# Feed-forward of a two-layer transformer block: the down product moved behind the next group's first gate and up

## The reference

```python
def swiglu_sublayer(h, shift, scale, gate, w_g, w_u, w_d, g, b):
    u = modulate(h, shift, scale)
    f = (jax.nn.silu(u @ w_g) * (u @ w_u)) @ w_d
    return post_norm(h, f, gate, g, b)
```

## Time and profile before

| | us |
|---|---|
| median of 3 runs | 4003.86 (4000.16 to 4005.01) |
| span of the profiled execution | 3998.6 |
| PE busy in it | 3531.9 (88%) |
| DVE, ACT, POOL busy | 1602.3, 1449.1, 1662.3 |
| matmuls of the feed-forward start, layer 0 | 1247.9 |
| matmuls of the feed-forward start, layer 1 | 3235.2 |

### The profile page before, as it was taken

The page is one execution under the profiler, slowest core; times in us unless marked ns, Lnnn a source line. Parts: engine busy times, 40 slices in busy tenths (PEclk is TensorE's granted clock), DMA queues, the critical chain, the costliest instruction groups (busy, mean ns, idle before and its releaser), DMA issues. The chain is left out here.

```text
span 3998.6 us, 55066 instructions
## 1 busy us (share of the span) xinstructions
PE 3531.9 (88%) x21518; PEld 2912.4 (73%) x21518; DVE 1602.3 (40%) x2560; ACT 1449.1 (36%) x2423; POOL 1662.3 (42%) x1104
## 2 busy tenths in 40 slices
PE   6899598788797999999998699597988979999997
PEld 2588487566476888888887487486665768888886
DVE  2103454686583222224433204465855722223324
ACT  2311275685443111113332311375854432222221
POOL 1211142583333444445565211244933345555553
PEclk9999799798998999999999799698989989999998
DMA  8422310232242222223333223322343433333332
GB/s 302 164 88 110 124 41 14 69 69 56 83 148 86 64 64 64 64 64 106 101 112 105 93 87 112 101 47 62 73 143 103 162 106 96 95 95 111 111 100 94
DMA packets 171083, 388.52 MB, mean 97 GB/s; under 512 B 14536, under 2 KB 75048, under 8 KB 170864
## 3 DMA queue, kind: packets, MB, share of 16 engines
q1 hardware_dynamic: 148480, 334.24, 27.3%
q10 hardware_dynamic: 19904, 44.77, 3.0%
q0 software_dynamic: 2480, 6.48, 0.6%
HBM read 319.41 MB, written 66.03 MB: 96 GB/s over the span
## 5 line engine op out<-in xcount | busy, mean ns | idle before, releaser
L2375 POOL TENSOR_TENSOR ffn_wlo<-ffn_raw,ffn_whi 128x1024 fp32r<-128x1024 f32 x264 | 644.5, 2448 | 677.1 <-ACT ffn_whi L2287 677.1
L2287 ACT CAST ffn_whi<-ffn_raw 128x1024 fp32r<-128x1024 f32 x264 | 272.6, 1049 | 877.2 <-PE ffn_acc L127 464.7
L2509 DVE TENSOR_TENSOR ffn_silu<-ffn_up,ffn_silu 128x256 f32<-128x256 f32 (+1 forms) x143 | 75.4, 527 | 946.3 <-PE ffn_up L127 937.0
L125 PE MATMUL ffn_gate<-second_uhi,ffn_whi 128*128 128x256 f32 (+1 forms) x1144 | 375.4, 328 | 42.8 <-POOL ffn_wlo L2375 34.1
L126 PE MATMUL ffn_gate<-second_ulo,ffn_whi 128*128 128x256 f32 (+1 forms) x1144 | 374.6, 327 | 0.0
L127 PE MATMUL ffn_gate<-second_uhi,ffn_wlo 128*128 128x256 f32 (+1 forms) x1144 | 374.3, 327 | 0.0
L125 PE MATMUL ffn_up<-second_uhi,ffn_whi 128*128 128x256 f32 (+1 forms) x1144 | 370.9, 324 | 0.8 <-POOL ffn_wlo L2375 0.8
L126 PE MATMUL ffn_up<-second_ulo,ffn_whi 128*128 128x256 f32 (+1 forms) x1144 | 370.6, 324 | 0.0
L127 PE MATMUL ffn_up<-second_uhi,ffn_wlo 128*128 128x256 f32 (+1 forms) x1144 | 370.3, 324 | 0.0
L2521 DVE TENSOR_TENSOR y<-ffn_acc,y 128x512 f32<-128x512 f32 x360 | 248.2, 691 | 257.8 <-PE ffn_acc L127 257.8
L125 PE MATMUL ffn_acc<-ffn_whi,ffn_hhi 128*128 128x512 f32 x792 | 314.1, 397 | 22.4 <-DVE y L2521 21.2
(11 more groups left out here) (286 smaller groups left out, 7939.2 us busy)
## 6 DMA issues: line engine op xcount, KB each, us to landing
ffn_raw<-w_ffn_dram SPq DMA_DIRECT2D x264, 512.0 KB, 3.6
in_raw<-w_in_dram SPq DMA_DIRECT2D x42, 512.0 KB, 3.6
inputs_ada_w<-w_ada_dram SPq DMA_DIRECT2D x10, 2048.0 KB, 8.3
swa_ada_w<-w_ada_dram SPq DMA_DIRECT2D x8, 2048.0 KB
proj_scratch<-in_stage ACTq DMA_DIRECT2D x20, 640.0 KB, 2.9
ada_w<-w_ada_dram SPq DMA_DIRECT2D x6, 2048.0 KB
gla_kq<-proj_scratch SPq DMA_DIRECT2D x32, 320.0 KB, 7.7
local_qhl<-heads_scratch SPq DMA_DIRECT2D x36, 256.0 KB
```

Source lines behind the costliest of these rows:

```text
L125: pe.matmul(out, st_hi, mv_hi, start=start, stop=False)
L2287: act.copy(whi[:, w % 3, :], raw[:, w % 2, :]).then_inc(w_hi, 1)
L2375: pool.tensor_tensor(wlo[:, w % 3, :], raw[:, w % 2, :], whi[:, w % 3, :].bitcast(F32), ALU.subtract).then_inc(w_ready, 1)
L2509: dve.tensor_tensor(sg[:, n % 2, 0:tn], UP[:, n % 2, 0:tn], sg[:, n % 2, 0:tn], ALU.mult).then_inc(mul_done, 1)
```

## The change

The loops over passes and groups become one loop over q = 0 to 21. On PE the down product of step q-1 moves behind G0 and U0 of step q and ahead of G1 and U1 of step q; the last one stands alone at the end. The order in which the weight tiles are loaded, split and kept in the three slots is now G0, U0, D0 and D1 of the step before, G1, U1 (`order`). The hidden tiles get three slots in place of two. `alone` goes: all chunks are whole. Each engine's loop is rewritten to that order. The core of the diff:

```diff
-        def alone(chunk):
-            t0, tn = chunk
-            return [[(t0, tn)], [(t0, tn // 2), (t0 + tn // 2, tn // 2)]]
-        passes = [alone(CHUNKS[0]) if last else [[CHUNKS[0], CHUNKS[2]]] * 2, alone(CHUNKS[1])]
...
+        passes = [[CHUNKS[0]] if last else [CHUNKS[0], CHUNKS[2]], [CHUNKS[1]]]
+        WIDTH = sum(tn for _, tn in passes[0])
+        Q = 2 * G
+        HS = 3
...
-        hhi = sb(nm + "hhi", [P, 2, WIDTH], F32R)
-        hlo = sb(nm + "hlo", [P, 2, WIDTH], F32R)
+        hhi = sb(nm + "hhi", [P, HS, WIDTH], F32R)
+        hlo = sb(nm + "hlo", [P, HS, WIDTH], F32R)
...
+        def hidden_slot(q, f):
+            return (2 * q + f) % HS
...
+        GATE, UPPER, DOWN = (0, 2), (1, 3), (4, 5)
+        order = []
+        for q in range(Q):
+            order += [(q, GATE[0]), (q, UPPER[0])]
+            if q:
+                order += [(q - 1, j) for j in DOWN]
+            order += [(q, GATE[1]), (q, UPPER[1])]
+        order += [(Q - 1, j) for j in DOWN]
+        place = {name: w for w, name in enumerate(order)}
...
-            for j in range(3):
-                split(0, 0, j)
-            for p in range(2):
-                for g in range(G):
-                    k = norm_tile(p, g)
-                    turning = k is not None and not last
-                    if k is not None:
-                        deviation(k, 0)
-                    if turning:
-                        deviation(k, 1)
-                    silu(p, g, 0)
-                    split(p, g, 3)
-                    if turning:
-                        normalize(k)
-                    split(p, g, 4)
-                    silu(p, g, 1)
-                    split(p, g, 5)
-                    if following(p, g)[0] < 2:
-                        split(*following(p, g), 0)
-                    if turning:
-                        if k == 0:
-                            act.wait_ge(one_plus, 1)
-                        modulate(k)
-                    if following(p, g)[0] < 2:
-                        for j in range(1, 3):
-                            split(*following(p, g), j)
+            split(0, GATE[0])
+            split(0, UPPER[0])
+            for q in range(Q):
+                k = norm_tile(q)
+                turning = k is not None and not last
+                if k is not None:
+                    deviation(k, 0)
+                if turning:
+                    deviation(k, 1)
+                silu(q, 0)
+                if q:
+                    split(q - 1, DOWN[1])
+                split(q, GATE[1])
+                if turning:
+                    normalize(k)
+                split(q, UPPER[1])
+                if q + 1 < Q:
+                    split(q + 1, GATE[0])
+                if turning:
+                    if k == 0:
+                        act.wait_ge(one_plus, 1)
+                    modulate(k)
+                silu(q, 1)
+                if q + 1 < Q:
+                    split(q + 1, UPPER[0])
+                split(q, DOWN[0])
+            split(Q - 1, DOWN[1])
...
-            for j in range(3):
-                split(0, 0, j)
-            for p in range(2):
-                for g in range(G):
-                    if not last and norm_tile(p, g - 1) is not None:
-                        low_part(norm_tile(p, g - 1))
-                    split(p, g, 3)
-                    hidden(p, g, 0)
-                    split(p, g, 4)
-                    split(p, g, 5)
-                    hidden(p, g, 1)
-                    if following(p, g)[0] < 2:
-                        for j in range(3):
-                            split(*following(p, g), j)
+            split(0, GATE[0])
+            split(0, UPPER[0])
+            for q in range(Q):
+                if not last and norm_tile(q - 1) is not None:
+                    low_part(norm_tile(q - 1))
+                if q:
+                    split(q - 1, DOWN[1])
+                split(q, GATE[1])
+                hidden(q, 0)
+                split(q, UPPER[1])
+                if q + 1 < Q:
+                    split(q + 1, GATE[0])
+                    split(q + 1, UPPER[0])
+                hidden(q, 1)
+                split(q, DOWN[0])
+            split(Q - 1, DOWN[1])
...
+            for q in range(Q):
+                gate_and_up(q, 0)
+                if q:
+                    down(q - 1)
+                if norm_tile(q) is not None and not last:
+                    turn(norm_tile(q))
+                gate_and_up(q, 1)
+            down(Q - 1)
```

## The result

The changed kernel takes 4038.14 us (median of 4 runs, 4033.99 to 4040.42), the kernel before 4003.20 us (4 runs). The ratio is 1.0085, with a 95% interval of 1.0072 to 1.0099: slower by 34.9 us. That lies in the predicted range (4044 us, 4020 to 4063, slower). The profiled execution has a span of 4035.2 us, 36.6 above that of before.

What follows compares the result with a forecast made beforehand. Plain steps were taken as bound by PE's matmul stream, norm steps partly by something else. Terms -21.8 - 3.7 + 38.1 + 7.2 + 20.4 = +40.2 us on the 3998.6 us span, plus 5.3 to the median, gave 4044; range 4020 to 4063.

Steps and rivals of the forecast that it cites:

- whole chunks: In 33 steps, 96 matmuls of 256 columns become 48 of 512; each step 0.66 us shorter, 21.8 us gained.
- hidden tile in pass 0: In pass 0 of layer 0, PE no longer waits for the hidden tile just made; 11 x 0.34 = 3.7 us gained.
- six norm steps of layer 0: Down product waits 6.5 or 9.3 us for D1's split, which stands behind norm work; three pairs lose 38.1 us.
- four norm steps of layer 1: PE waits 1.8 us for D1's split in each of four steps, no clock loss charged; 7.2 us lost.
- two ends: Each layer's last down product waits 7.8 us for POOL, plus 2.4 us of clock; twice 10.2 = 20.4 us lost.
- Plain steps don't wait: In steps without norm work the weights arrive in time, with 1.0 us to spare for D1; steps of 32.64 us.
- rival (a): DVE's norm chain gets 2 us shorter, so ten norm steps wait less: 19 us back, 4025; chance 0.14.
- The clock: Behind long waits PE's clock falls to the 1.2 GHz level; 2.2 us lost in a norm step, 2.4 at an end.
- The transposes: Waits ahead of the transposes in norm steps of layer 0 cost 1.2 us a step, as before.
- (d): Rival for whole chunks: wider matmuls save nearly nothing, 17.5 us worse, 4062; chance 0.06 together with another rival.
- (b): Rival for norm steps: silu comes early enough that the norm chain doesn't hold D1; -28 us, 3976; chance 0.05.

Runs made afterwards that it cites:

- d1_cast_first: Changed kernel with D1's cast on ACT ahead of the step's square roots and silu, in place of behind them; 4005.15 us, ratio to the kernel before 1.0005.
- filler: Changed kernel with matmuls whose result nobody reads run on PE ahead of the eight long waits for D1; 4021.82 us, ratio to the kernel before 1.0043.
- tail_splits_first: Changed kernel with D0 and D1 split on POOL ahead of the hidden tile in each layer's last step; 4023.80 us, ratio to the kernel before 1.0046.
- before_whole: Kernel before with the second hidden tile in one piece of 512 columns, the down product not moved; 4128.27 us, ratio to the kernel before 1.0309.

## Why the prediction was right

In the feed-forward parts the change costs 34.8 us; the other 1.8 of the profile's 36.6 lie in stages it doesn't touch. The mechanism and the time both came out as forecast; two terms were off by 2 to 4 us. Point by point:

| term | predicted | measured in the trace |
|---|---|---|
| whole chunks, 33 x 0.66 | -21.8 | 0.66 in every plain step |
| hidden tile in pass 0, 11 x 0.34 | -3.7 | 0.31 to 0.33 a step |
| six norm steps of layer 0 | +38.1 | +34.7 |
| four norm steps of layer 1 | +7.2 | +5.1 |
| two ends | +20.4 | +20.9 |

The last three are against steps of 32.64 us; with 33 x 0.66 and 11 x 0.32 for the first two, the terms add up to 35.4 us, 0.6 above the 34.8. For layer 0 the six steps are 64.0 us over 32.64 now and were 29.3 over 33.30; the ends are 78.8 us from U1's end to the next stage's first matmul against 68.1, and 49.3 against 39.1.

- Plain steps don't wait: right. PE is never idle in them, and D1 is there in time.
- Norm steps: the mechanism is right and shown (d1_cast_first). The waits are 5.97 (once 6.76) and 8.35 us between matmuls, I had 6.5 and 9.3; in layer 1 1.04 (once 1.31), I had 1.8. The term was taken from the split in the same place of the kernel before. The difference is part of rival (a): DVE's second `residual` operation takes 1.52 us now, 3.30 before, and `shifted` then meets D0's split and takes 2.91, where 1.66 stood before. In the second step the low part of the normed tile falls on `shifted` (3.22 us for 1.29), against 2.9 us saved in `residual`. The chain came out 0.5 to 1.0 us shorter, not 2. In layer 1 the whole wait of 1.04 us is D1's split itself: it starts at 3662.91, behind a DVE operation that started at 3662.79, and takes 3.40 us where it takes 2.4 elsewhere.
- The clock: it fell in all eight long waits, 2.33 to 2.65 us in a norm step's down product, I had 2.2, and didn't fall after 0.88 us. The filler run shows it as a cost of its own.
- The transposes cost 0.9 us in a norm step and not the 1.2 that I took over from the kernel before.
- The ends: 7.62 us of wait in place of 7.8, shown by tail_splits_first.
- The matmul's cost: (d) is out. 144 matmuls of 512 take 32.64 us, so the gain is that of the rows. The 4.3 us came from the formula of the Trainium skill (TensorE: Matmul & The Clock Gate, Back-to-back issue gap), which that section gives for a single matmul by itself; the trace doesn't agree with it for this stream. But (d) had a grain of truth from another side: whole chunks are worth only 8.5 us in the new order, since they make the hidden tile late where it counts.
- (b) needed D1 6 us earlier. When its cast is moved, it comes that early in the first step of a pair (and 3.2 us too late in the second), yet the time is 4005, not the 3976 of (b): the accumulators are next in line, and my prediction named no wait behind D1.
- The range: with the two terms that I named for the lower end taken together, 18 us for the clock and 19 for the chain, it would start at 4007 and not at 4022. The measured time doesn't test this.

## What to carry to other kernels

When an operand is handed from engine to engine, look for the longest queue that it stands in at its worst step, not at the plain one: moving work behind a buffer's next use put one weight behind a chain that had cost little before. A split that several matmuls wait for belongs ahead of work that waits for another engine; here four changes of order, none of them taking work away, turned 0.9% slower into 0.8% faster. No run gives the kernel before such an order of work, so how much of the 0.8% the moved down product brings is open. And count the clock with each wait of several microseconds; here it added 2.4 us to waits of 6 and 8.

## What the hardware showed that I had not expected

- Two matmuls of 256 columns take 240 ns and one of 512 takes 226.7 in the same stream; 0.66 us in every plain step.
- The clock doesn't always fall after a wait of about 3 us. In before_whole most down products behind a wait of 3.08 us take 12.6 us, a few 11.0; in d1_cast_first three of the six waits of 3.1 to 3.3 us in norm steps had no fall behind them; in tail_splits_first it fell two or three matmuls after PE was running again. After each wait of 4.3 us and more in the feed-forward parts of these runs the granted clock was 0.50.
- DVE's operations with two SBUF inputs of 128x1024 take 1.22 to 1.29 us in the tail, with POOL idle, and 1.52, 2.91 or 3.22 us beside an operation of POOL, depending on which of the two came first; the other way round POOL's split goes from 2.4 to 3.40 us. This is in line with the exclusive lock that the Trainium skill describes (SBUF — State Buffer, SBUF: two separate sides). So a split on POOL delays ACT's silu by way of DVE's norm work, though nothing in the code joins them.
